# A router that reads the residual itself, and picks its experts with max8 and match-replace, in an encoder layer on one core

## The chip, the cores and the metric

The kernel runs on one core of a Trainium2 chip. The metric is the device time in microseconds (us), the median of a few runs. The engines are TensorE (PE; its weight loads are listed as PEld), VectorE (DVE), ScalarE (ACT), GpSimd (POOL) and SyncE (SP), which here issues all the transfers.

## The reference

One encoder layer over 256 tokens of width 1024: an input projection, a convolution branch and a windowed attention branch, their gated sum, an output projection, and a layer norm; then a mixture of experts and a second layer norm. The change lies at the border between the two halves:

```python
x = layer_norm(DEEPNORM_ALPHA * x + mixed, ln1_g[l], ln1_b[l])
...
g_logits = (t @ w_rg + b_rg).astype(jnp.float32)          # 4 groups
g_prob = jax.nn.softmax(g_logits, axis=-1)
g_idx = jnp.argmax(g_logits, axis=-1)
g_w = jnp.take_along_axis(g_prob, g_idx[:, None], axis=-1)
e_logits = (t @ w_re + b_re).astype(jnp.float32).reshape(-1, N_GROUPS, EXPERTS_PER_GROUP)
e_in = jnp.take_along_axis(e_logits, g_idx[:, None, None], axis=1)[:, 0]
e_prob = jax.nn.softmax(e_in, axis=-1)
top_w, top_i = lax.top_k(e_prob, TOP_K)                   # 2 of the group's 8 experts
top_w = top_w / top_w.sum(-1, keepdims=True)
weight = g_w * top_w
...
for e in range(N_EXPERTS):                                # 32 experts, hidden width 256
    hg, hu = jnp.split(t @ w_gate_up[e], 2, axis=-1)
    out = out + comb[:, e:e + 1] * ((jax.nn.silu(hg) * hu) @ w_down[e])
```

## The kernel before

**Blocks.** The first half is a loop over 72 weight blocks of 128x1024, each loaded by SP into one of four `raw` buffers: 48 of the input projection, 8 each of the attention, convolution and output projections. ScalarE rounds a block to fp32r (`w_hi`, L567), POOL subtracts that from the block (`w_lo`, L502), both in halves of 512 columns into two buffers, and TensorE makes three products for each pair of tiles (hi x hi, hi x lo, lo x hi; L1250 to L1252). VectorE takes finished pairs of blocks out of PSUM. For a convolution pair it multiplies by the gate (L893), adds the attention branch (L897); ScalarE rounds the sum (`a_hi`, L597), in its queue ahead of the split of the next block, and VectorE makes `a_lo` (L899). The eight output blocks (64 to 71) add to four PSUM banks, `out_bank`, into which VectorE has put alpha times the residual (L990). They hold two token tiles t by two column halves c.

**Layer norm and logits.** VectorE takes moments of each bank (L994, L997), ScalarE the root (L675), and the normalised rows z go from the banks to `xt` (L1011 on VectorE, L684 on ScalarE). TensorE turns them (L1412), ScalarE and VectorE copy the result (L679, L1024) and TensorE makes 36 logits a token with router weights scaled by the norm's gain (L1418). Eight products of ones with the shift-scaled weights (L1402) add the shift's part. ScalarE rounds z to `x1_hi` (L693), POOL makes `x1_lo` (L511).

**Routing.** VectorE runs a chain in which each step waits for the one before (`chained`): largest group, the first of equals by a descending key, a mask for other groups, the largest expert by the same five steps (`first_of_largest`), then the second. The sum of the two one-hots (L1070, `onehot_done`) goes to TensorE, which counts for each token how many before it chose each expert, with a strict upper triangle `tri` and a matrix of ones (L1443 to L1447, fp32). From these ranks come each token's place in its expert's list, a 0/1 matrix that gathers the first four experts' tokens (L1079), the weights, the sort of all 512 (token, expert) entries (`compact`), and the start of each expert's list. Then `load_known` releases POOL, which turns z into x1 (L517, L520). `keep_warm` issues products of ones with constants whose results nobody reads.

**Experts.** Sixteen pairs of experts, windows of 64 tokens each: gather (first four experts L1458, the others from the sorted copy), gate-up (L1498), silu (L717), h (L1162), transposes of h (L1522), down (L1533), scatter into `out_bank` (L1548). `build_gather` (L1132, L1137) and `build_scatter` (L1169) on VectorE make 0/1 matrices. SP refills seven homes of gate-up weights and four of down weights as products release them.

## Time and profile before

| What | us |
|---|---|
| Median of 3 runs (lowest, highest) | 487.08 (486.75, 487.19) |
| The profiled execution's own time | 486.77 |
| Its span | 484.6 |
| TensorE busy | 467.1 |
| VectorE busy | 245.6 |
| ScalarE busy | 202.4 |
| POOL busy | 223.2 |
| Last output product ends | 236.25 |
| First gather instruction | 252.53 |
| TensorE's time for a pair of experts, from the chain | 12.94 |

The span runs from the first to the last instruction. In a timeline, a row has the start, the time, the engine, the line, the operation, out<-in, the shapes, the count, and in brackets the idle time before it with what ended it; a matmul's time has its latency in it, so the distance between starts is what one costs. A fp32 product is two instructions. A row of the windows has the stretch, its length, the busy time with count of PE, PEld, DVE, ACT and POOL, then TensorE's granted clock as a share of 2.4 GHz, the DMA engines' busy share and GB/s. Durations of a line are least/median/greatest in ns.

### The profile page before, as it was taken

The numbers are of one execution on the slowest core, as the hardware profiler recorded it, in microseconds if no ns is written. First come the engines' busy times: TensorE is split into PE (matmuls) and PEld (weight loads), VectorE is DVE, ScalarE is ACT, GpSimd is POOL, SyncE is SP. The second block draws the span as 40 slices with busy tenths as digits, with TensorE's granted clock in tenths as the row PEclk, the third lists the DMA queues.
The fourth block names the chain that finished last, engine by engine and source line by source line (L and its number), as shares of the span: only waits on it lengthen the run. The fifth ranks groups of instructions, "written<-read, shape, count | busy, mean of one in ns | idle before, by whom it ended". The sixth has DMA issues, their size and how long they took to land.

```text
span 484.6 us, 7686 instructions
## 1 busy us (share of the span) xinstructions
PE 467.1 (96%) x2816; PEld 329.7 (68%) x2816; DVE 245.6 (51%) x536; ACT 202.4 (42%) x447; POOL 223.2 (46%) x187
## 2 busy tenths in 40 slices
PE   8999999999999999999998999999999999999991
PEld 6999999888999999998884464443334444444431
DVE  2079999759997546560469442222222222222116
ACT  3544455488775687454425241212122222222212
POOL 2898989855866778999235321110001111111002
PEclk9999999999999999999999999999999999999996
DMA  8799989532533354557974999999999999999922
GB/s 291 257 355 378 354 284 360 193 131 88 194 131 121 121 168 156 199 174 277 428 292 164 395 419 381 427 422 421 420 422 421 422 420 422 421 421 421 421 97 88
DMA packets 26370, 145.13 MB, mean 299 GB/s; under 512 B 3040, under 2 KB 3296, under 8 KB 13792
## 3 DMA queue, kind: packets, MB, share of 16 engines
q1 hardware_dynamic: 26336, 144.67, 75.9%
q8 instruction: 23, 0.38, 0.3%
q14 instruction: 11, 0.09, 0.1%
HBM read 143.61 MB, written 1.05 MB: 298 GB/s over the span
## 4 chain that ended last, share of the span: by engine, by line
PE 86%; DVE 6%; ACT 3%; DMA 2%; issue 1%; SPq 1%; POOL 1%; DVEq 0%; ACTq 0%
PE bank L1498 21%; PE bank L1250 13%; PE bank L1252 13%; PE bank L1251 13%; PE bank L1533 12%; PE bank L1548 3%; PE bank L1549 3%; DMA raw<-in_w_in 2%; PE bank L1328 1%; PE bank L1306 1%; PE bank L1522 1%; DVE info L1137 1%; POOL w_lo L502 1%; PE bank L1472 1%; PE bank L1473 1%
## 5 line engine op out<-in xcount | busy, mean ns | idle before, releaser
L502 POOL TENSOR_TENSOR w_lo<-raw,w_hi 128x512 fp32r<-128x512 f32 x140 | 183.1, 1326 | 46.8 <-ACT w_hi L567 43.3
L567 ACT CAST w_hi<-raw 128x512 fp32r<-128x512 f32 x140 | 85.2, 620 | 80.1 <-PE bank L1252 75.6
L1250 PE MATMUL bank<-x_hi,w_hi 128*128 128x256 f32 x400 | 115.4, 289 | 1.3 <-POOL w_lo L502 1.3
L1252 PE MATMUL bank<-x_hi,w_lo 128*128 128x256 f32 x400 | 113.1, 283 | 0.0
L1251 PE MATMUL bank<-x_lo,w_hi 128*128 128x256 f32 x400 | 113.1, 283 | 0.0
L813 DVE SCALAR_TENSOR_TENSOR bank<-slots,par,bank 128x256 f32<-128x256 f32 x232 | 92.3, 481 | 0.2
L528 POOL COPY raw<-gates 128x512 f32 x28 | 19.8, 706 | 153.1 <-PE bank L1498 134.6
L1498 PE MATMUL bank<-slots,raw 128*64 128x512 f32 x320 | 84.5, 592 | 0.0
L1250 PEld LDWEIGHTS bank<-x_hi,w_hi 128*128 128x128 f32 x400 | 76.6, 192 | 2.0 <-issue 1.3
L1251 PEld LDWEIGHTS bank<-x_lo,w_hi 128*128 128x128 f32 x400 | 76.7, 192 | 0.3
L1252 PEld LDWEIGHTS bank<-x_hi,w_lo 128*128 128x128 f32 x400 | 76.7, 192 | 0.0
L1533 PE MATMUL bank<-slots,kT 128*64 128x512 f32 x256 | 58.5, 598 | 0.4 <-ACT kT L723 0.4
L1498 PEld LDWEIGHTS bank<-slots,raw 128*64 128x64 f32 x320 | 27.5, 137 | 44.8 <-issue 44.4
L1162 DVE SCALAR_TENSOR_TENSOR pT<-pT,kT,bank 128x256 f32<-128x256 f32 x16 | 7.7, 481 | 89.6 <-ACT pT L717 89.6
L1176 DVE TENSOR_TENSOR w_lo<-bank,w_hi 128x512 fp32r<-128x512 f32 x32 | 22.1, 691 | 57.2 <-ACT w_hi L730 57.2
L717 ACT ACTIVATE pT<-bank 128x256 f32<-128x256 f32 x16 | 6.1, 384 | 94.2 <-PE bank L1498 94.2
L1533 PEld LDWEIGHTS bank<-slots,kT 128*64 128x64 f32 x256 | 17.2, 136 | 28.3 <-issue 28.1
L730 ACT CAST w_hi<-bank 128x512 fp32r<-128x512 f32 x32 | 18.8, 586 | 36.8 <-PE bank L1533 36.8
L1548 PE MATMUL bank<-w_hi,w_lo 128*128 128x512 f32 x64 | 28.2, 440 | 1.2 <-DVE gates L1183 0.9
L1498 PE MATMUL bank<-spare,raw 128*64 128x512 f32 x64 | 28.1, 592 | 0.0
L1498 PE MATMUL bank<-extra,raw 128*64 128x512 f32 x64 | 28.1, 592 | 0.0
L1498 PE MATMUL bank<-late,raw 128*64 128x512 f32 x64 | 28.1, 592 | 0.0
(213 smaller groups left out, 657.1 us busy)
## 6 DMA issues: line engine op xcount, KB each, us to landing
slots<-in_w_gate_up SPq DMA_DIRECT2D x40, 1024.0 KB, 13.2
slots<-in_w_down SPq DMA_DIRECT2D x32, 1024.0 KB, 13.8
raw<-in_w_in SPq DMA_DIRECT2D x48, 512.0 KB, 4.3
extra<-in_w_gate_up SPq DMA_DIRECT2D x8, 1024.0 KB, 13.2
spare<-in_w_gate_up SPq DMA_DIRECT2D x8, 1024.0 KB, 16.1
late<-in_w_gate_up SPq DMA_DIRECT2D x8, 1024.0 KB, 16.3
raw<-in_w_attn SPq DMA_DIRECT2D x8, 512.0 KB, 3.2
raw<-in_w_conv SPq DMA_DIRECT2D x8, 512.0 KB, 3.3
```

Of the source, the lines that this page charges most:

```text
L502: nc.gpsimd.tensor_tensor(w_lo[:, n % SPLIT, m], raw[:, b % RAW, m], w_hi[:, n % SPLIT, m].bitcast(F32), ALU.subtract).then_inc(w_lo_done, 1)
L528: ins = nc.gpsimd.tensor_copy(xg[u][:, :, j * WIN:(j + 1) * WIN], xgT[:, :, bass.ds(at, WIN)])
L567: nc.scalar.copy(w_hi[:, n % SPLIT, m], raw[:, b % RAW, m]).then_inc(w_hi_done, 1)
L730: nc.scalar.copy(y_hi[:, c * HALF:(c + 1) * HALF], y_bank[c][:]).then_inc(y_hi_done, 1)
L813: ins = nc.vector.scalar_tensor_tensor(dst, h_pad[:, i, tap:tap + SEQ], w, so_far, ALU.mult, ALU.add)
L1176: nc.vector.tensor_tensor(y_lo[:, n], y_bank[c][:], y_hi[:, n].bitcast(F32), ALU.subtract).then_inc(y_lo_done, 1)
L1250: mm(dst, ah, bh, start=first, stop=False, **kw)
L1251: mm(dst, ah, bl, start=False, stop=False, **kw)
L1252: return mm(dst, al, bh, start=False, stop=last, **kw)
L1498: ins = mm(gu_bank[j * WIN:(j + 1) * WIN, :], xg[u][:, k, j * WIN:(j + 1) * WIN], weights(j, k // (KT // 2), k % (KT // 2) == 0)[:, n], st ...
L1533: ins = mm(y_bank[c][j * WIN:(j + 1) * WIN, :], hT[:, k, j * WIN:(j + 1) * WIN], w[:, k, c * HALF:(c + 1) * HALF], start=(k == 0), stop=(k ...
L1548: mm(dst, s, y_hi[:, n], start=False, stop=False, skip_group_check=True)
```

## The change

- The logits are made from the residual sum r itself: the column mean of each scaled router column is taken out of the weights (sums on VectorE, two small products, a subtraction), the shift's part goes into the bias, and VectorE multiplies the logits by each token's inverse deviation. ScalarE copies r from the banks to `xt`; TensorE turns r; ScalarE alone normalises, afterwards. L1402 goes.
- Experts are chosen with one max8 and one match-replace for each token tile. The groups' key is scaled to serve as the mask. Many of the small operands are in PSUM.
- The ranks are products of fp32r operands: two for the ranks of both token tiles, two for the totals.
- The first gather matrix and the first gather go by token tile. The sort moves behind the weights and the first two `build_gather`.
- The constants that this needs (fp32r copies of `tri` and ones, the token numbers in `info`, filling values) are set by VectorE before block 63's pair is taken. Of the warm-up products, 3 at the start stay, 17 become 6.

```diff
-WARM_START, WARM_NORM, WARM_TURN, WARM_ROUTE, WARM_PLACE = 3, 2, 1, 11, 2
+WARM_START, WARM_ROUTE, WARM_PLACE = 3, 5, 1
...
             for t in range(TT):
...
+                for c in range(2):
+                    m = slice(c * HALF, (c + 1) * HALF)
+                    pool.wait_ge(x1_hi_done, 2 * t + c + 1)
+                    nc.gpsimd.tensor_tensor(x1_lo[:, t, m], xt[:, t, m], x1_hi[:, t, m].bitcast(F32),
+                                            ALU.subtract).then_inc(x1_lo_done, 1)
+            pool.wait_ge(x1_lo_done, 2 * TT)
+            pool.wait_ge(gat_built, 2)
             pool.wait_ge(load_known, 1)
...
+            def copy_r(n, t, c):
+                act.wait_ge(out_done, n + 1)
+                nc.scalar.copy(xt[:, t, c * HALF:(c + 1) * HALF], out_bank[2 * t + c][:]).then_inc(r_copied, 1)
+            def copy_rT(n, c):
+                act.wait_ge(r_turned, n + 1)
+                nc.scalar.copy(x1T[:, 4 * c:4 * c + 4, 0:P],
+                               turned_bank[n][:].rearrange("p (a t) -> p a t", a=4)).then_inc(rT_by_act, 1)
+            def normalize_rows(t, c):
+                act.wait_ge(z_shift, t + 1)
+                nc.scalar.activation(xt[:, t, c * HALF:(c + 1) * HALF], out_bank[2 * t + c][:], ACT.Identity,
+                                     scale=mv[:, t, 3:4], bias=mv[:, t, 4:5]).then_inc(z_done, 1)
+            def split_x1(t, c):
+                m = slice(c * HALF, (c + 1) * HALF)
+                nc.scalar.copy(x1_hi[:, t, m], xt[:, t, m]).then_inc(x1_hi_done, 1)
+            nc.scalar.activation(sig[:, 0, 0:1], eps[:, 0:1], ACT.Sqrt)
+            for n, (t, c) in enumerate(((0, 0), (1, 0), (0, 1), (1, 1))):
+                copy_r(n, t, c)
             deviation(0)
...
+            copy_rT(0, 0)
             deviation(1)
...
+            copy_rT(2, 1)
             for t in range(TT):
...
+                if t == 1:
+                    act.wait_ge(r_turned, 2 * TT)
+                for c in range(2):
+                    normalize_rows(t, c)
+                    act.wait_ge(z_done, 2 * t + c + 1)
+                    split_x1(t, c)
             act.wait_ge(exp_in, 1)
+            for t in range(TT):
+                nc.scalar.activation(rt[:, 7, t, :], masked[:, t, 0:EXPERTS], ACT.Exp, bias=rs[:, 2, t:t + 1])
...
+                    chained(nc.vector.tensor_tensor(wr[:], wr[:], per_channel[0], ALU.mult))
+                    for a, w in enumerate((wr[:], bias_wr)):
+                        ins = nc.vector.tensor_reduce(wr_sums[:, a, :], w.rearrange("p k n -> p n k"), X_AXIS, ALU.add)
+                    ins.then_inc(wr_summed, 1)
+                if b == B_CONV - 2:
+                    dve.wait_ge(wr_means_done, 1)
+                    nc.vector.tensor_tensor(wr[:], wr[:], wr_bank[:, 0, :].unsqueeze(1).broadcast_to([P, KT, LOGITS]),
+                                            ALU.subtract)
+                    nc.vector.tensor_tensor(row[:, R_BIAS:R_BIAS + LOGITS], row[:, R_BIAS:R_BIAS + LOGITS],
+                                            wr_bank[:, 1, :], ALU.add).then_inc(wr_ready, 1)
+                if b == B_OUT - 2:
+                    nc.vector.memset(needles, NO_LOGIT)
+                    nc.vector.memset(masked[:, :, EXPERTS:], NO_LOGIT)
+                    for u in range(2):
+                        for n in (0, 5):
+                            nc.vector.tensor_copy(info[u][:, :, n:n + 1], con[:, C_TOKEN:C_TOKEN + TT].unsqueeze(2))
+                    nc.vector.tensor_copy(tri_r, tri)
+                    nc.vector.tensor_copy(ones_r, ones[:]).then_inc(sums_ready, 1)
+                    dve.wait_ge(sums_ready, 1)
                 if b == B_VAR:
...
             for n, (t, c) in enumerate(((0, 0), (1, 0), (0, 1), (1, 1))):
...
+                dve.wait_ge(r_copied, n + 1)
+                moments(t, c, xt[:, t, c * HALF:(c + 1) * HALF])
+            def copy_rT(n, c):
+                dve.wait_ge(r_turned, n + 1)
+                nc.vector.tensor_copy(x1T[:, 4 * c:4 * c + 4, P:2 * P],
+                                      turned_bank[n][:].rearrange("p (a t) -> p a t", a=4)).then_inc(rT_by_dve, 1)
+            copy_rT(1, 0)
             inverse(0)
...
+            shift(0, z_shift)
+            copy_rT(3, 1)
             inverse(1)
...
+            shift(1, z_shift)
             def per_token(col, n):
                 return col.unsqueeze(2).broadcast_to([P, TT, n])
...
             dve.wait_ge(logits_done, 1)
...
+            for t in range(TT):
+                ins = nc.vector.scalar_tensor_tensor(lg[:, t, :], logit_bank[:, t, :], mv[:, t, 3:4],
+                                                     row[:, R_BIAS:R_BIAS + LOGITS], ALU.mult, ALU.add)
+            chained(ins)
             g_log = lg[:, :, 0:GROUPS]
...
             chained(nc.vector.tensor_reduce(rs[:, 0, :], g_log, X_AXIS, ALU.max))
+            for t in range(TT):
+                ins = nc.vector.scalar_tensor_tensor(group_key[:, t, :], g_log[:, t, :], rs[:, 0, t:t + 1], rank4,
+                                                     ALU.is_equal, ALU.mult)
+            chained(ins)
+            chained(nc.vector.tensor_reduce(rs[:, 1, :], group_key, X_AXIS, ALU.max))
+            def grouped(a):
+                return a.rearrange("p (g e) -> p g e", g=GROUPS)
+            for t in range(TT):
+                ins = nc.vector.scalar_tensor_tensor(
+                    grouped(masked[:, t, 0:EXPERTS]), group_key[:, t, :].unsqueeze(2).broadcast_to([P, GROUPS, PER_GROUP]),
+                    rs[:, 1, t:t + 1], grouped(lg[:, t, GROUPS:]), ALU.subtract, ALU.add)
+            chained(ins)
+            for t in range(TT):
+                ins = nc.vector.max(largest[:, t, :], masked[:, t, 0:EXPERTS])
+            chained(ins)
+            chained(nc.vector.tensor_copy(needles[:, :, 0:2], largest[:, :, 0:2]))
+            for t in range(TT):
+                ins = nc.vector.match_replace(marked[:, t, :], needles[:, t, :], masked[:, t, :], NEVER)
+            chained(ins)
+            nc.vector.tensor_scalar(onehot, marked[:, :, 0:EXPERTS], NEVER, None, ALU.is_equal).then_inc(onehot_done, 1)
+            nc.vector.tensor_scalar(rs[:, 2, :], largest[:, :, 0], -1.0, None, ALU.mult)
             nc.vector.tensor_tensor(rg[:, 0, :, :], g_log, per_token(rs[:, 0, :], GROUPS),
...
+            chosen = onehot.bitcast(F32)
+            rank = bank[4][:, 0:TT * EXPERTS].rearrange("p (t n) -> p t n", t=TT)
+            place = rt[:, 0, :, :]
             dve.wait_ge(onehot_done, 1)
             dve.wait_ge(ranks_done, 1)
...
+            chained(nc.vector.scalar_tensor_tensor(first_place, rank[:, :, 0:4], 1.0, chosen[:, :, 0:4], ALU.add, ALU.mult))
+            for t in range(TT):
+                nc.vector.tensor_tensor(
+                    first_places[:, t, :].rearrange("p (j s) -> p j s", j=4),
+                    iota[:, 0:WIN].unsqueeze(1).broadcast_to([P, 4, WIN]),
+                    first_place[:, t, :].unsqueeze(2).broadcast_to([P, 4, WIN]), ALU.is_equal).then_inc(first_built, 1)
+            nc.vector.scalar_tensor_tensor(place, rank, 1.0, chosen, ALU.add, ALU.mult)
+            dve.wait_ge(router_exp, 1)
+            nc.vector.tensor_reduce(rs[:, 6, :], rg[:, 1, :, :], X_AXIS, ALU.add)
+            chained(nc.vector.tensor_tensor(rt[:, 6, :, :], chosen, rt[:, 7, :, :], ALU.mult))
+            chained(nc.vector.tensor_reduce(rs[:, 9, :], rt[:, 6, :, :], X_AXIS, ALU.add))
...
             def build_gather(p, u):
@@ -1199,6 +1217,33 @@
             build_gather(0, 0)
             build_gather(1, 1)
+            dve.wait_ge(ranks_done, 2)
...
+            for t in range(TT):
+                if t == 0:
+                    chained(nc.vector.tensor_reduce(load_f[:], rt[0:1, 9, 0, :], X_AXIS, ALU.max))
+                nc.vector.scalar_tensor_tensor(compact[:, t, :], iota, rs[:, 14, t:t + 1], first_choice[:, t, :],
+                                               ALU.is_equal, ALU.add).then_inc(compact_built, 1)
+            for w in range(WINDOWS + 1):
+                nc.vector.tensor_scalar(starts_f[:, w, :], rt[0:1, 9, 1, :], float(WIN * w), float(ROUTED),
+                                        ALU.add, ALU.min)
+            chained(nc.vector.tensor_copy(load_i[:], load_f[:]))
+            nc.vector.tensor_copy(starts[:], starts_f).then_inc(load_known, 1)
+            dve.wait_ge(load_known, 1)
...
+                if b == B_VAR + 3:
+                    pe.wait_ge(p_copied, HEADS)
+                    pe.wait_ge(wr_summed, 1)
+                    mm(wr_bank[:, 0, :], mean_ones[:], wr_sums[:, 0, :], start=True, stop=True)
+                    mm(wr_bank[:, 1, :], ones[:], wr_sums[:, 1, :], start=True, stop=True).then_inc(wr_means_done, 1)
+            pe.wait_ge(wr_ready, 1)
...
+            def turn_r(n, t, c):
+                pe.wait_ge(r_copied, n + 1)
                 for i in range(4):
...
+                    at = 4 * c + i
+                    ins = nc.tensor.transpose(turned_bank[n][:, i * P:(i + 1) * P], xt[:, t, at * P:(at + 1) * P], ident)
+                ins.then_inc(r_turned, 1)
...
+            turn_r(0, 0, 0)
+            turn_r(1, 1, 0)
+            turn_r(2, 0, 1)
+            pe.wait_ge(rT_by_act, 1)
+            turn_r(3, 1, 1)
             logits(0, 0)
...
+            pe.wait_ge(rT_by_dve, 1)
+            logits(1, 0)
+            pe.wait_ge(rT_by_act, 2)
             logits(0, 1)
...
+            pe.wait_ge(rT_by_dve, 2)
             logits(1, 1).then_inc(logits_done, 1)
             keep_warm(bank[1][:, 0:SEQ], WARM_ROUTE)
...
+            pe.wait_ge(sums_ready, 1)
+            pe.wait_ge(z_done, 2 * TT)
             pe.wait_ge(onehot_done, 1)
...
+            mm(bank[4][:, 0:TT * EXPERTS], tri_r, onehot.rearrange("p t n -> p (t n)"), start=True, stop=False,
+               skip_group_check=True)
+            mm(bank[4][:, EXPERTS:TT * EXPERTS], ones_r, onehot[:, 0, :], start=False, stop=True,
+               skip_group_check=True).then_inc(ranks_done, 1)
+            mm(bank[5][:, 0:EXPERTS], ones_r, onehot[:, 0, :], start=True, stop=False)
+            mm(bank[5][:, 0:EXPERTS], ones_r, onehot[:, 1, :], start=False, stop=True).then_inc(ranks_done, 1)
+            keep_warm(bank[2][:, 0:SEQ], WARM_PLACE, iota[:, 0:SEQ])
...
+                for t in range(TT):
+                    pe.wait_ge(x1_lo_done, 2 * t + 2)
+                    pe.wait_ge(first_built, t + 1)
+                    for k in range(KT):
+                        n = slice(k * P, (k + 1) * P)
+                        dst = first_bank[k // 2][:, (k % 2) * SEQ:(k % 2 + 1) * SEQ]
```

Of long stretches the diff shows the lines that are new or stay; the removed ones stand in the functions above. Not shown either: the places of the new small tensors, the names of semaphores, the last norm, whose moments keep their banks.

## Rows read from the trace of the kernel before

**Rows 1.** The page: the chain that ended last, shares of the span by engine.
```profile
PE 86%; DVE 6%; ACT 3%; DMA 2%; issue 1%; SPq 1%; POOL 1%; DVEq 0%; ACTq 0%
```
**Rows 2.** Windows of the first gather and gate-up; columns as told above.
```profile
252.53:256.53 4.00, 4.00 (x32) 3.87 (x33) 3.52 (x17) 2.77 (x6) 0.00 (x0) 1.00 0.00 0
256.53:263.64 7.11, 7.11 (x34) 2.30 (x33) 6.97 (x22) 2.62 (x5) 3.69 (x2) 1.00 0.32 106
```
**Rows 3.** Timeline of TensorE, 236 to 266 us; columns as told above.
```profile
237.82 1.08 PE L1335 MATMUL bank<-pT,ones 128*128 128x256 f32 x4
238.74 1.04 PE L1412 MATMUL bank<-con,xt 128*128 128x128 f32 x8
...
243.09 1.87 PE L1418 MATMUL bank<-wr,raw 128*128 128x36 f32 x16
244.80 5.00 PE L1335 MATMUL bank<-pT,ones 128*128 128x256 f32 x22
250.02 0.41 PE L1443 MATMUL bank<-rt,con 128*128 128x32 f32 x2 [0.23 <-DVE rt L1070]
...
265.65 0.44 PE L1522 MATMUL bank<-con,pT 128*128 128x128 f32 x2 [1.72 <-DVE pT L1162]
```
**Rows 4.** Timeline of VectorE, routing stretch.
```profile
245.56 0.17 DVE L1039 TENSOR_TENSOR bank<-bank,rs 128x8 f32<-128x8 f32 x1
245.76 0.17 DVE L1040 TENSOR_TENSOR bank<-bank,con 128x8 f32<-128x8 f32 x1
...
246.84 0.22 DVE L1058 TENSOR_REDUCE rs<-rt 128x2 f32<-128x64 f32 x1
247.09 0.22 DVE L1059 TENSOR_TENSOR rt<-rt,rs 128x64 f32<-128x64 f32 x1
...
251.43 0.23 DVE L1077 SCALAR_TENSOR_TENSOR rt<-bank,rt 128x64 f32<-128x64 f32 x1 [1.36 <-PE bank L1447]
```
**Rows 5.** Timeline of ScalarE, routing stretch.
```profile
237.67 0.78 ACT L684 ACTIVATE xt<-bank,mv 128x512 f32<-128x512 f32 x1 [0.79 <-DVE mv L1006]
...
239.37 1.07 ACT L679 COPY raw<-bank 128x512 f32<-128x512 f32 x2 [0.75 <-PE bank L1412]
240.68 0.59 ACT L679 COPY raw<-bank 128x512 f32<-128x512 f32 x1 [0.23 <-PE bank L1412]
...
243.18 1.28 ACT L695 ACT_TABLE_LOAD   x1
```
**Rows 6.** POOL's x1 passes and VectorE beside them; durations of line 511.
```profile
259.95 5.12 POOL L517 TENSOR_TENSOR xt<-xt,gates 128x1024 f32<-128x1024 f32 x2 [12.99 <-DVE starts L1123]
...
260.13 2.40 DVE L1137 CAST info<-weights 128x4 fp32r<-128x4 f32 x2
...
L511 POOL TENSOR_TENSOR x_lo<-xt,x_hi x2: 2348/2352/2357, 242.3 to 244.6; 128x1024 fp32r<-128x1024 f32 x2
```
**Rows 7.** Timelines of VectorE and TensorE around the router scaling and block 55.
```profile
172.23 0.69 DVE L887 TENSOR_TENSOR gates<-bank,gates 128x512 f32<-128x512 f32 x1 [3.12 <-PE bank L1252]
...
187.77 0.39 PE L1250 MATMUL bank<-a_hi,w_hi 128*128 128x256 f32 x1 [0.72 <-POOL w_lo L502]
```
**Rows 8.** Timelines of VectorE and POOL before block 64.
```profile
206.43 1.27 DVE L990 TENSOR_SCALAR bank<-xt 128x512 f32<-128x512 f32 x2
208.67 0.69 DVE L893 TENSOR_TENSOR gates<-bank,gates 128x512 f32<-128x512 f32 x1 [0.97 <-PE bank L1252]
...
212.04 4.06 POOL L502 TENSOR_TENSOR w_lo<-raw,w_hi 128x512 fp32r<-128x512 f32 x3 [0.16 <-ACT w_hi L567]
```
**Rows 9.** Windows: loads in the pair stage, in the gather, at the end.
```profile
300.00:322.00 22.00, 22.00 (x104) 8.76 (x104) 5.69 (x13) 5.05 (x17) 2.26 (x3) 1.00 1.01 422
...
252.00:258.00 6.00, 5.73 (x42) 4.51 (x42) 5.45 (x22) 4.22 (x9) 0.00 (x0) 1.00 0.00 0
...
460.00:464.00 4.00, 4.00 (x22) 1.38 (x20) 0.69 (x1) 0.43 (x1) 0.00 (x0) 1.00 0.81 338
```
**Rows 10.** Window after the last product; timeline of TensorE at the start.
```profile
476.70:484.60 7.90, 0.00 (x0) 0.00 (x0) 5.28 (x11) 1.14 (x3) 2.53 (x2) 0.50 0.36 133
...
4.03 1.87 PE L1347 MATMUL bank<-pT,ones 128*128 128x256 f32 x4
```

229 lines of the change are left out of this document (59 added, 170 removed).

## The prediction

> **What bounds the kernel now.** I first read the page: 86% of the chain that ended last runs on TensorE and 6% on VectorE [rows 1]. Then the windows by stage: TensorE is full in all of them [rows 2], also between 236.25 and 252.53 us. TensorE's timeline shows that this is misleading there: it runs 22 + 4 + 2 + 2 + 4 warm-up instructions (two of the five groups stand in the rows) whose results nobody reads [rows 3]. What really sets that stretch is in VectorE's timeline, which is where its 6% of the chain come from: one small dependent step after another [rows 4]. So TensorE bounds the kernel up to 236.25 (last output product) and again from 252.53 (first gather), and in between lies a serial stretch of 16.28 us. Everything after it hangs on its end: gather 4.00, first gate-up 7.11 [rows 2], then a short wait of 1.72 us before the transposes of h [rows 3], and from there TensorE with next to no idle time. What the change takes out of the 16.28 us therefore comes out of the span, unless another queue is late.
>
> **1. From the last product to the logits.** Before: variance, square root, normalised rows, transposes, logits; VectorE takes the logits at 245.00. After: ScalarE copies the four raw blocks (a PSUM copy is 0.59 us [rows 5]), the fourth from about 236.3 to 236.9. TensorE turns three groups meanwhile (0.44 us each, 1.04 for two with the drain [rows 3]), until 237.6. The fourth needs bank 0 back: moments of the third block (some 0.65 us each in its timeline) end near 236.9, the variance is there at 237.15, ScalarE does the root (0.28) and the copy of the first group (0.59 [rows 5]) until 238.0. Fourth group 238.0 to 238.45. Then the 32 logit instructions, 0.108 us apart (1.87 for sixteen with the drain [rows 3]), 3.45 us, drain 0.2: VectorE starts at 242.1. Gain 2.9. Bounds: if TensorE never waits, 236.25 + 1.75 + 3.45 + 0.2 = 241.65, gain 3.35; if ScalarE's queue is late by one copy and one root, gain 2.0.
>
> **2. The choice.** Before, 245.00 to 250.02: 5.02 us [rows 3, 4]. A dependent step of 8 elements costs 0.20, one of 64 costs 0.26, and a second independent one adds 0.08 to 0.15 [rows 4]. After: logits (a pair) 0.34, group maximum 0.20, key pair 0.28, its maximum 0.20, masked pair 0.33, one-hot 0.25: 1.60 us. Not in this trace: the max8 pair, the copy of two values, the match-replace pair. Lower bound: all three at the price of small steps, 0.28 + 0.20 + 0.28 = 0.76. Upper: ten dependent 64-element steps, 2.5, so that each of the seven instructions stands alone and half of them cost double. I take 1.15 (a reduction of 64 is the nearest row; I count the replace as two instructions each). Together 2.75: onehot at 244.85, gain 2.3 (0.9 to 2.65).
>
> **3. The ranks.** Before, 250.02 to 251.43: ten instructions for five fp32 products, some 0.112 apart [rows 3, 4]. After, VectorE waits for two one-pass products only: 1.41 - 8 x 0.112 = 0.51. Gain 0.9; if each product still were two instructions, 0.7.
>
> **4. First places.** Before, 251.43 to 252.53: 1.10 (all 64 places, then 128x512 in 0.69 us). After: 8 elements 0.22, then 128x256 in 0.40 (L1132 in VectorE's timeline, the same comparison at that size), hand-over 0.08: 0.7. Gain 0.4. The second half is built while TensorE does the first 16 products.
>
> Sum: 2.9 + 2.3 + 0.9 + 0.4 = **6.5 us**; the gather starts near 246.0.
>
> **What could be late next.** ScalarE must normalise and split four halves before TensorE may write the ranks: 4 x (0.78 + 0.6) [rows 5] from 239.05 puts the fourth normal row at 244.0, 0.85 before onehot; its price if slower is one for one. POOL's low parts (a half is 1.16, half of the 2.35 of [rows 6]) end near 245.7, and are needed for the second half of the gather at 248.0. The exponentials (table 1.28, three of 0.2 [rows 5]) end at 246.4; VectorE waits some 0.3 us for them, after the places. ScalarE's first gathered copy comes later (all groups close in the second half, 248.5) but 2 x 0.49 us later is 249.5, before TensorE ends the gather at 250.0. The sort and the token starts, moved behind the weights and the two gather matrices, keep VectorE until about 254.6; h needs it at 265.11 - 6.5 = 258.6. So they are off the path, with 4 us of cover. POOL's four passes over x1, held behind load_known, start near 254.5 instead of 259.95 [rows 6]; the masks they hold up are needed only after the second gate-up.
>
> **5. Work added further up.** The router sums and column means: two reductions of 288 elements after the scaling at 169.1. The nearest rows bound each by 0.22 [rows 4] and 1.43 (L974, 288 elements); VectorE then idles 3.12 us until 172.23 [rows 7]. Hidden; without that cover, up to 2.9. The four small TensorE instructions near 178 (0.45 us) fall ahead of a stall of 0.7 us on TensorE, caused by ScalarE and POOL [rows 7]. Subtracting the means takes under 1 us in VectorE's next idle stretch. Cost 0.
>
> **6. The eight small instructions before block 63.** This is where I expect a loss. Two memsets, four casts of 128x2, and copies of two 128x128 matrices come after VectorE's residual scaling, which ends at 207.70. VectorE next takes a pair of blocks at 208.67, with 0.97 us idle before it [rows 8]. Own time of the eight: 0.75 us. But POOL runs its 1.3 us subtractions back to back. In the gather stretch, two casts of 128x4 took 2.40 us, ending when POOL's 2.56 us pass ended [rows 6], and the next two 2.38; when POOL is idle the pair takes 0.23. So VectorE's copies wait for POOL's running instruction and get a short burst in between. VectorE's lateness goes to the merge at L897, to ScalarE, which holds block 64's split behind a_hi (L597), to POOL's start at 212.04 on block 64, to TensorE at 214.43. POOL's first subtraction there is done 1.08 us before TensorE needs it. With one wait for POOL the merge is 0.3 us later: nothing. With two, 1.9: a stall of 0.9. With three, 2.9: a stall of 1.8; more there cannot be, as POOL has only three subtractions left until ScalarE feeds it. TensorE can't win it back (2.73 us a block against POOL's 2.65). I take two waits, **0.9** (0 to 1.8).
>
> **Rivals.**
> - *As computed*, 481.5, own range 480.4 to 483.0: 0.57.
> - *No stall in part 6*: 487.08 - 6.5 = 480.6. For it: the 0.97 us gap and 1.08 us of slack. Against: the casts. 0.18.
> - *The gain is capped by the expert loads.* The DMA engines are full during the pair stage (share 1.01, and 14.9 us for 6.29 MB at 422 GB/s against 12.94 us of TensorE a pair) [rows 9] (12.94 is how often the chain repeats). If the loads did not move up, only their margin would be won: the last ones land near 463.2, the last down product starts at 469.02; about 5.1 for the gate-up halves ahead of them in the queue, so 482.0. Against: between 252 and 260.2 the DMA engines stand still, and every refill waits for a product that moves up too. 0.05.
> - *VectorE is late for h* because the sort now stands before it: only what exceeds 4 us counts, say 483. 0.03.
> - *TensorE's clock falls for a while.* Of the 34 warm-up instructions 22 are gone, 20 of them between the last product and onehot. The granted clock is 1.00 (2.4 GHz) throughout and 0.50 (1.2 GHz) from 476.7, 4.1 us after the last product [rows 10]; at the half rate an instruction of 256 columns took 0.43 (the start of the run) instead of 0.22 [rows 3, 10]. If it fell at the end of the logits, the ten warm-ups would end at 246.2 instead of 244.1, 1.4 late, and half of the gather would double (+2.0), the whole +4.0. Time 484.9 to 486.9, I take 485.2. The Trainium skill (TensorE: Matmul & The Clock Gate, section "Part 4: PE-mode transpose") says that transposes do not bring the full clock; the trace can't show it, since they have warm-ups among them here. 0.12.
> - *The same, but the clock stays low through the first gate-up*: 1.4 + 4.0 + 7.1 = 12.5 us lost, 6.9 slower net of the gain, 494. It decides from the point where the low clock costs 5.6: the whole gather and over 0.2 us of gate-up. For it: TensorE's gaps of about 0.4, 0.7 and 0.5 us; against: it is never idle for long, and the kernel before kept 1.00 through a gap of 1.72. 0.05.
>
> **Numbers.** The first four cases hold 0.83, between 479.7 (parts 1 and 2 at their best and no stall: 479.8) and 485.2, where the low-clock case begins to weigh; that is the range. Faster by over 0.2%: 0.83 and nine tenths of 0.12: 0.93. Within 0.2%: 0.02. Slower: 0.05.
>
> **What would show it.** First logits instruction on VectorE near 5.8 us after the last product's end (8.75 before); onehot 2.75 after that; places 0.5 after onehot; gather about 9.8 after the last product (16.28 before); the 1.72 us wait before the first transposes of h unchanged; clock row at 1.00 in all of it; a TensorE stall of about 0.9 at block 64, its releaser POOL. The prediction is wrong if that stall exceeds 2 us, if max8 and match-replace together cost over 2.5, or if the clock row falls.

## The result, and the profile after

| What | before | after |
|---|---|---|
| Median, us (lowest to highest, runs) | 487.58 (486.72 to 489.40, 20) | 485.17 (483.43 to 487.13, 20) |
| Ratio, 95% interval | | 0.9947 (0.9937 to 0.9958) |
| Span of the profiled execution | 484.6 | 482.9 |
| Last upstream product over, next instruction starts | 236.09 | 239.83 |
| First logits instruction on VectorE | 245.00 | 246.01 |
| First rank product | 250.02 | 249.48 |
| First gather instruction | 252.53 | 250.85 |

The change makes the kernel faster by 0.53% (0.42 to 0.63), 2.6 us, of the 5.6 forecast (2.6 goes by the ratio; the two medians lie 2.4 apart). The forecast time of 481.5 is 3.7 below the median; 0.5 of that comes from before's own median, which was 487.08 in the three runs of the forecast and is 487.58 in twenty. The stretch behind the last upstream product did shrink, from 16.44 to 11.02 us between the starts of its first instruction and of the gather, but it begins 3.74 us later. (The prediction counts from 236.25, where the chain has the end of the product; below it is always the start of the next instruction, 236.09.)

**The routing stretch.** The page's chain by engine now has half the share of VectorE that it had [rows 1]:
```profile
PE 90%; DVE 3%; ACT 3%; DMA 1%; issue 1%; POOL 1%; DVEq 0%; SPq 0%; ACTq 0%
```
TensorE's timeline after the last product, to be laid beside [rows 3]:
```profile
239.83 1.47 PE L1455 MATMUL bank<-con,xt 128*128 128x128 f32 x12
241.75 0.66 PE L1455 MATMUL bank<-con,xt 128*128 128x128 f32 x4 [0.45 <-ACT raw L703]
242.25 3.66 PE L1461 MATMUL bank<-wr,raw 128*128 128x36 f32 x32
245.74 4.09 PE L1380 MATMUL bank<-pT,ones 128*128 128x256 f32 x10
249.48 0.38 PE L1481 MATMUL bank<-onehot,sums 128*128 128x64 f32 x1
```
Three groups of raw transposes, a wait of 0.45 for bank 0, the fourth group, 32 logits instructions: 6.18 us to VectorE's first step, where it was 8.91. Then ten warm-up instructions take 4.09 us; at the full clock ten take 2.40 (in before_few_warm's profile). They are the first sign of something that the forecast's sum puts at zero.

VectorE's timeline of the choice and the hand-over to the ranks, against [rows 4]:
```profile
246.01 0.43 DVE L1089 SCALAR_TENSOR_TENSOR bank<-bank,mv,row 128x36 f32<-128x36 f32 x2 [2.53 <-PE bank L1461]
246.47 0.17 DVE L1093 TENSOR_REDUCE rs<-bank 128x2 f32<-128x8 f32 x1
...
247.70 0.29 DVE L1109 MAX8 bank<-rt 128x8 f32<-128x32 f32 x2
248.03 0.16 DVE L1111 COPY rt<-bank 128x4 f32<-128x4 f32 x1
248.22 0.09 DVE L1113 MATCH_VALUE_LOAD bank<-rt 128x8 f32 x1
248.30 0.19 DVE L1113 MATCH_REPLACE8 bank<-rt 128x40 f32<-128x40 f32 x1
...
248.70 0.23 DVE L1115 TENSOR_SCALAR onehot<-bank 128x64 fp32r<-128x64 f32 x1
...
250.07 0.17 DVE L1125 SCALAR_TENSOR_TENSOR bank<-bank,onehot 128x8 f32<-128x8 f32 x1 [1.01 <-PE bank L1483]
```
The new instructions are cheap: both maxima, the copy and both replacements run from 247.70 to 248.70. One-hot is done at 248.93, 2.92 after the first step; with the hand-over TensorE could have started at 3.05 (the kernel late_consts_warm_logits, where it waits for one-hot, shows that). It starts at 249.48 since the warm-ups ahead of the rank products in its queue are still running.

The windows of the routing, the gather and the first gate-up [rows 2]:
```profile
239.83:250.85 11.02, 10.43 (x66) 9.05 (x64) 7.03 (x32) 9.42 (x18) 5.06 (x4) 0.85 1.01 424
250.85:254.85 4.00, 4.00 (x34) 3.87 (x34) 3.62 (x21) 1.34 (x3) 0.00 (x0) 1.00 0.85 352
254.85:262.00 7.15, 7.15 (x35) 2.34 (x34) 3.68 (x16) 3.89 (x8) 3.06 (x2) 1.00 0.35 113
```
Gather and gate-up cost what they did, 4.00 and 7.15 us. The mean clock of the first stretch is 0.85; a finer window shows where it goes:
```profile
244.00:246.00 2.00, 2.00 (x19) 2.00 (x19) 0.00 (x0) 1.97 (x4) 1.83 (x2) 0.96 1.00 422
246.00:249.50 3.50, 3.50 (x11) 2.76 (x10) 2.77 (x18) 3.41 (x6) 3.23 (x3) 0.54 1.01 414
```
From 245.84 on TensorE is granted 1.2 GHz, half, for 3.41 us: the choice's warm-ups and nothing else. In before's profiled execution it had 2.4 GHz up to its last product.

**Where the 3.74 us come from.** Part of it was there from the beginning. Groups of TensorE in the first 25 us, of after, and of the same kernel in another profiled execution (after_again):
```profile
L1317 PE MATMUL bank<-gates,raw 128*128 128x256 f32 x32 | 9.0, 450 | 0.7 <-DMA raw<-in_w_in 0.7
```
```profile
L1317 PE MATMUL bank<-gates,raw 128*128 128x256 f32 x32 | 7.2, 382 | 0.8 <-DMA raw<-in_w_in 0.8
```
The same 32 instructions take 1.8 us more in one execution of one and the same kernel. At block 55 after is 1.41 us behind before (189.18 against 187.77, [rows 7]), after_again 0.23: that is the start, and no part of the change. The rest, 3.74 - 1.41 = 2.33 us, arises at block 64. VectorE's and POOL's timelines of after, which answer to [rows 8] (w_lo x3 are the three subtractions on block 64):
```profile
207.85 1.27 DVE L1047 TENSOR_SCALAR bank<-xt 128x512 f32<-128x512 f32 x2
209.09 1.27 DVE L1028 CAST info<-con 128x2 fp32r<-128x2 f32 x1
209.12 0.07 DVE L1024 MEMSET rt<- 128x16 f32 x1
209.13 0.07 DVE L1025 MEMSET rt<- 128x16 f32 x1
210.28 1.42 DVE L1028 CAST info<-con 128x2 fp32r<-128x2 f32 x3
211.61 1.33 DVE L1029 CAST sums<-con 128x128 fp32r<-128x128 f32 x1
212.86 0.21 DVE L1030 CAST sums<-ones 128x128 fp32r<-128x128 f32 x1
213.11 0.69 DVE L930 TENSOR_TENSOR gates<-bank,gates 128x512 f32<-128x512 f32 x1
```
```profile
215.83 4.68 POOL L517 TENSOR_TENSOR w_lo<-raw,w_hi 128x512 fp32r<-128x512 f32 x3 [2.98 <-ACT w_hi L585]
```
And TensorE's first product of block 64, in before and in after:
```profile
214.23 0.40 PE L1250 MATMUL bank<-w_hi,a_hi 128*128 128x512 f32 x1
```
```profile
217.25 0.47 PE L1295 MATMUL bank<-w_hi,a_hi 128*128 128x512 f32 x1 [1.45 <-POOL w_lo L517]
```
Six casts and copies that together are worth some 0.6 us fill 4.0 us: three of them end a POOL subtraction later than they could. The two memsets between them take 0.07 each. The Trainium skill (SBUF — State Buffer, section "Who interferes with whom") has copies and casts in a two-port mode waiting while GpSimd holds the ports that they share, and an instruction outside these modes with at most one input from SBUF, as a memset is, not waiting; the rows agree with both halves. VectorE takes the pair of blocks at 213.11; less the 1.41 of the start that is 3.0 later than the 208.67 of before. POOL's three subtractions on block 64 start 2.4 later by the same count and take 4.68 instead of 4.06 us.

### The profile page after: what moved, and what is told of

Same layout as the page of the kernel before. It is cut to its first block, busy times and chain, and to the rows that moved or that the text cites. A ratio compares the mean times of both kernels' runs of the same rounds, so it can differ in the third digit from the quotient of the medians.

```text
span 482.9 us, 7627 instructions
## 1 busy us (share of the span) xinstructions
PE 464.1 (96%) x2776; PEld 326.1 (68%) x2776; DVE 242.2 (50%) x538; ACT 207.2 (43%) x457; POOL 222.9 (46%) x189
## 4 chain that ended last, share of the span: by engine, by line
PE 90%; DVE 3%; ACT 3%; DMA 1%; issue 1%; POOL 1%; DVEq 0%; SPq 0%; ACTq 0%
PE bank L1539 23%; PE bank L1295 13%; PE bank L1297 12%; PE bank L1296 12%; PE bank L1574 12%; PE bank L1589 4%; PE bank L1590 3%; PE bank L1317 2%; PE bank L1373 1%; PE bank L1351 1%; DMA raw<-in_w_in 1%; PE bank L1563 1%; DVE stat L1051 1%; POOL w_lo L517 1%; PE bank L1380 1%
```

## The experiments

All of them were run with five rounds beside the kernel before. "Last product" is where the instruction after the last upstream product starts, less the lag at block 55 against before (187.77), so that the start of the execution is out of it: before has 236.09, after 238.42, a stall of 2.33.

**1. late_consts.** The change, with the eight instructions moved behind VectorE's work on the last block.
```diff
-                if b == B_OUT - 2:
-                    nc.vector.memset(needles, NO_LOGIT)
...
-                    nc.vector.tensor_copy(ones_r, ones[:]).then_inc(sums_ready, 1)
-                    dve.wait_ge(sums_ready, 1)
+            dve.wait_ge(w_lo_done, 2 * splits_before(N_BLOCKS))
+            nc.vector.memset(needles, NO_LOGIT)
...
+            nc.vector.tensor_copy(ones_r, ones[:]).then_inc(sums_ready, 1)
+            dve.wait_ge(sums_ready, 1)
```

> The changed kernel, but VectorE's eight small instructions (two memsets, four casts, two 128x128 copies) no longer stand before block 63's pair; they run after the block loop, once POOL has made its last low part, and nothing else differs. Theory (VectorE's casts wait for POOL's running subtraction, three in a row, and ScalarE holds block 64's split behind the merge): TensorE's two stalls at blocks 64 and 65 (1.4 and 1.1 us) go, the output product ends some 2.3 us earlier counted from the first split block, and the ratio to the kernel before goes from 0.9947 to about 0.990. Rival (the stall has another cause, such as the w_out loads or the router means further up): the stalls stay and so does the ratio, 0.9947.

483.04 us, ratio 0.9914 (0.9889 to 0.9939). Its last product is at 236.21 - 0.16 = 236.05: the stall is gone to the last tenth. (The second stall of 1.1 us that the expectation puts at block 65 is the one that ends at 121.0; it is in before as well, at 119.60.) VectorE's timeline at the new place, where POOL has no subtraction left:
```profile
233.49 0.15 DVE L1044 CAST info<-con 128x2 fp32r<-128x2 f32 x1
233.50 0.07 DVE L1041 MEMSET rt<- 128x16 f32 x1
233.54 0.30 DVE L1044 CAST info<-con 128x2 fp32r<-128x2 f32 x3
233.75 0.22 DVE L1045 CAST sums<-con 128x128 fp32r<-128x128 f32 x1
```
The same instructions take what their size costs. The median is 2.1 below that of after, by the ratios it is 1.6, and their intervals just overlap (0.9939 and 0.9937); the row of the last product is the surer sign. The clock is no better here, as two windows show:
```profile
240.90:247.60 6.70, 6.70 (x24) 5.86 (x23) 2.77 (x18) 5.32 (x10) 4.67 (x4) 0.50 1.01 416
247.70:251.00 3.30, 3.16 (x25) 2.79 (x24) 2.63 (x13) 0.00 (x0) 0.00 (x0) 1.00 0.98 407
```
Here the clock is at half for the second half of the logits and all of the choice. The 32 logits instructions took 4.81 us, against 3.66 at the full clock in after.

**2. before_with_consts.** The kernel before with nothing but the eight instructions, in the change's place.
```diff
...
+                if b == B_OUT - 2:
+                    nc.vector.memset(spare_rt[:, 0:16], 0.0)
+                    nc.vector.memset(spare_rt[:, 16:32], 0.0)
+                    for u in range(2):
+                        for n in (0, 5):
+                            nc.vector.tensor_copy(info[u][:, :, n:n + 1], con[:, C_TOKEN:C_TOKEN + TT].unsqueeze(2))
+                    nc.vector.tensor_copy(sums_sb[:, 0, :], tri)
+                    nc.vector.tensor_copy(sums_sb[:, 1, :], ones[:]).then_inc(sums_ready, 1)
+                    dve.wait_ge(sums_ready, 1)
```

> The kernel before with only those eight instructions added before block 63's pair (their results are not used). Theory: they alone cost 2.3 us, ratio 1.0047, with VectorE's casts lasting to the ends of POOL's subtractions and TensorE stalled at block 64. Rival (they only hurt together with the rest of the change): ratio 1.000.

490.70 us, ratio 1.0057 (1.0036 to 1.0078), 2.8 us slower. Last product 238.75 - 0.34 = 238.41: a stall of 2.32, with nothing else of the change there. So the stall belongs to these eight instructions alone, and nothing behind it wins it back: the interval of the time is 1.8 to 3.8 us. The profiled execution also has 3.41 us at half the clock from 269.13 on, behind the wait of 1.72 us ahead of the transposes of h, which before's own profile has not.

**3. four_casts_early.** The change with only the four casts in that place; memsets and the two 128x128 copies stand late as in experiment 1.

> The changed kernel with only the four casts of the information rows left ahead of block 63; the three memsets-and-copies of the 128x128 constants stand behind the block loop. Theory A (each cast or copy on VectorE that falls between POOL's pieces waits for one of them, and the run of POOL pieces is what is late for TensorE): two POOL waits instead of three, the last upstream product ends 0.7 to 1.2 us later than without any of them (the changed kernel: 2.3), ratio to the kernel before 0.991 to 0.993. Theory B (any instruction in that place costs the whole stall, because VectorE then comes behind the next POOL piece): stall 2.3 as in the changed kernel, ratio 0.995. Theory C (the copies are what costs, since they read and write more): stall 0 to 0.4, ratio 0.990.

483.87 us, ratio 0.9923 (0.9900 to 0.9946). VectorE's timeline:
```profile
206.46 1.27 DVE L1042 TENSOR_SCALAR bank<-xt 128x512 f32<-128x512 f32 x2
207.65 2.60 DVE L1026 CAST info<-con 128x2 fp32r<-128x2 f32 x4
210.16 0.68 DVE L930 TENSOR_TENSOR gates<-bank,gates 128x512 f32<-128x512 f32 x1
```
and TensorE's:
```profile
214.77 0.47 PE L1297 MATMUL bank<-w_hi,a_hi 128*128 128x512 f32 x1 [0.36 <-POOL w_lo L517]
```
Two waits, and a last product at 237.20 - 0.02 = 237.18: a stall of 1.09. No wait gives 0, two give 1.1, three 2.3 (one alone was not run). The number of waits decides (A); not the place alone (B), and not the copies alone (C).

**4. after_again.** The changed kernel once more, on the same chip as 3, 7 and 8.

> The changed kernel itself, unchanged, on the same chip as the others. Ratio to the kernel before 0.993 to 0.996; TensorE waits for POOL's w_lo pieces 3.0 to 3.5 us in the block loop; whether the clock is full early in the span or some 4 us later should move its span by about 1.4 us; if the late start belongs to the change, it will be late here too, and if it is chance, it can be at 5 to 6 us.

484.31 us, ratio 0.9933 (0.9910 to 0.9956), consistent with the first comparison. Last product 238.70 - 0.23 = 238.47: stall 2.38. Its start was the early one, its clock fell too, for 3.41 us from 245.05. So the late start differs between executions of one kernel, and the other two losses came in both profiles.

**5. before_few_warm.** The kernel before with the change's numbers of warm-up products.
```diff
-WARM_START, WARM_NORM, WARM_TURN, WARM_ROUTE, WARM_PLACE = 3, 2, 1, 11, 2
+WARM_START, WARM_NORM, WARM_TURN, WARM_ROUTE, WARM_PLACE = 3, 0, 0, 5, 1
```

> The kernel before with the changed kernel's number of warm-up products and nothing else: none around the norm and the transposes, five after the logits, one after the ranks. Clock theory (with few products among transposes and narrow logits the granted clock falls near the end of the logits): the clock row shows under 1.00 between 240 and 252 us, warm-ups of 0.43 us an instruction, and where the fall reaches the gather some us are lost; ratio 1.000 to 1.008. Removing 10 of them from the way before the logits saves up to 0.9 us by itself, ratio 0.998, if the clock stays. Rival (the fall in the changed kernel comes from its order of work, not from the number of warm-ups): clock 1.00 throughout.

489.14 us, ratio 1.0031 (1.0015 to 1.0048). Windows of its choice and gather:
```profile
248.00:252.00 4.00, 1.82 (x12) 1.41 (x12) 2.40 (x11) 0.20 (x1) 0.00 (x0) 1.00 0.72 297
252.00:255.40 3.40, 3.35 (x16) 3.39 (x17) 2.95 (x15) 1.02 (x2) 0.00 (x0) 0.50 0.01 2
255.40:258.00 2.60, 2.60 (x21) 2.18 (x22) 2.53 (x9) 2.28 (x5) 0.00 (x0) 1.00 0.00 0
```
TensorE stood idle for 2.97 us before the ranks, and the clock falls in the gather: 16 instructions in 3.4 us where the next 2.6 us have 21. Fewer warm-ups do cost the clock, in the old kernel as well: six of the twelve runs have a mean clock of 0.982 to 0.986, where the lowest of the 18 runs of before beside them is 0.989. The time is 1.5 us longer (0.7 to 2.3).

**6. late_consts_warm_logits.** Experiment 1 with three single warm-up products: one in the 0.45 us wait ahead of the fourth transposes, two among the logits.
```diff
             turn_r(2, 0, 1)
+            keep_warm(bank[7][:, SEQ:2 * SEQ], 1)
             pe.wait_ge(rT_by_act, 1)
...
             logits(1, 0)
+            keep_warm(bank[1][:, 0:SEQ], 1)
             pe.wait_ge(rT_by_act, 2)
             logits(0, 1)
+            keep_warm(bank[1][:, 0:SEQ], 1)
             pe.wait_ge(rT_by_dve, 2)
```

> The kernel of late_consts with three warm-up products more: one in TensorE's 0.45 us gap before the fourth group of transposes, two among the logits. They lengthen the way to the logits by 0.9 us. Clock theory: if three are enough, the clock row stays at 1.00, the ten warm-up instructions after the logits take 2.2 instead of 4.1 us, TensorE is ready before onehot, and the loss of 0.9 is partly given back (0.5): ratio 0.4 us above late_consts, with less spread between runs. Rival (the clock has nothing to do with it or three are too few): the clock falls all the same and the ratio is 0.9 us, 0.002, above late_consts.

483.13 us, ratio 0.9900 (0.9882 to 0.9919), and the narrowest spread so far: 482.90 to 483.50 in five runs, against 482.58 to 485.53 in experiment 1. Its windows:
```profile
236.20:248.00 11.80, 10.72 (x75) 9.26 (x74) 7.47 (x35) 9.42 (x18) 5.09 (x4) 1.00 1.01 421
262.00:266.00 4.00, 4.00 (x12) 1.39 (x10) 4.00 (x5) 0.87 (x3) 3.50 (x3) 0.57 1.02 426
```
Full through the routing, and low for 3.41 us after the next wait, the 1.77 us ahead of the first transposes of h.

**7. late_consts_route3.** Experiment 1 with 3 instead of 5 warm-up products in the choice (6 instructions instead of 10).

> late_consts with 3 warm-up products in place of 10 between the logits and the choice's result. Theory A (the ten products at the low clock run past the choice and hold the ranks up by about half a us, and the clock is bought back by nothing they do): the rank products start when onehot is there, 0.3 to 0.6 us sooner, ratio 0.989 to 0.991. Theory B (those products keep the clock up for the gather): TensorE is idle some 1.5 us there, the low stretch comes in the gather or the transposes of h, the time is the same as late_consts or up to 1.5 us longer, ratio 0.991 to 0.995.

485.03 us, ratio 0.9932 (0.9908 to 0.9955): worse than experiment 1 by 2.0 us in the medians and by 0.9 in the ratios, whose intervals overlap. Seven of its eight runs have a mean clock of 0.983 to 0.985; experiment 1 has 0.984 to 0.991. Windows:
```profile
243.00:253.00 10.00, 9.55 (x37) 8.29 (x37) 6.78 (x39) 4.84 (x9) 4.16 (x4) 0.50 0.96 396
253.00:256.00 3.00, 3.00 (x22) 2.32 (x23) 2.82 (x10) 2.21 (x5) 0.00 (x0) 1.00 0.02 8
```
The ranks did start sooner, 3.05 us after VectorE's first step instead of 3.75. But the low stretch is now 10.24 us long and takes most of the gather with it. Theory A, that those products do nothing but stand in the ranks' way, does not hold. (The 10 in this expectation and in the first one of experiment 8 counts instructions, which are 5 products; the 3 and the 7 beside it count products.)

**8. late_consts_filled**, and once more on another chip as **late_consts_filled_again**. Experiment 6 with 7 products in the choice and three in the wait ahead of the transposes of h.
```diff
-WARM_START, WARM_ROUTE, WARM_PLACE = 3, 5, 1
+WARM_START, WARM_ROUTE, WARM_PLACE = 3, 7, 1
...
             slot_info(0, 0)
+            keep_warm(bank[2][:, 0:SEQ], 3, iota[:, 0:SEQ])
             for p in range(PAIRS):
```

> late_consts_warm_logits with 7 warm-up products in place of 10 in the choice and 3 more in the 1.8 us in which TensorE waits ahead of the transposes of h. Theory A (the low stretch at 262 us comes from the idle time just before it): no stretch at 0.5 until the end, the transposes of h and the first gate-up products take 1 to 1.7 us less, span 480.0 to 480.6, ratio 0.987 to 0.989. Theory B (the low stretch is not tied to that gap): there is one at another place, and the ratio stays at 0.990 as in late_consts_warm_logits.

> late_consts_filled once more, on the chip of the two kernels beside it. Ratio 0.987 to 0.990; the runs in two groups about 1.4 us apart if the clock at the start decides, the lower one at 481.8, the larger.

481.90 us, 0.9889 (0.9866 to 0.9913), and 481.64 us, 0.9888 (0.9868 to 0.9907). Both profiles have no stretch at half the clock before the last product. The window that was at 0.57:
```profile
262.00:266.00 4.00, 4.00 (x20) 1.55 (x18) 4.00 (x5) 1.46 (x4) 3.59 (x3) 1.00 1.04 432
```
20 instructions in the same 4 us instead of 12. The low stretch came from the wait just before it, and the runs agree: 481.4 to 482.0 in eight of twelve, the other four 482.8 to 483.1, as the two starts would have it.

**9. before_gap_filled.** The kernel before with those three products ahead of the transposes of h.

> The kernel before with one addition: 3 warm-up products in the 1.7 us in which TensorE waits ahead of the first transposes of h. Theory A (the runs of the kernel before near 488.2 to 488.8 us are those in which the clock falls at that wait, those near 486.9 the ones in which it does not): nearly all runs at 486.6 to 487.1, ratio 0.997 to 0.998. Theory B (the upper group comes from the start of the kernel, where the clock becomes full some 4 us later in some executions, at a price of 1.4 to 1.6 us): both groups stay, ratio 0.999 to 1.001.

487.05 us, ratio 0.9988 (0.9976 to 1.0001). The runs lie in two groups as those of the kernel before do: 486.6 to 487.5 (9 runs) and 488.1 to 488.5 (3), against 486.5 to 487.0 (6) and 488.1 to 488.9 (11). Fewer in the upper group, but the group is not gone, so the late start (B) is one cause of it. This profile is such a case: the first 32 products took 8.9 us, there was no low stretch after them, and the last product was at 237.46.

Theory A is not out altogether. Of the 59 runs of the kernel before that were taken beside these experiments 18 have a mean clock of 0.989 or less, and all 18 lie above 488.4; of the 12 filled runs none is under 0.992. A mean of 0.989 is, as an estimate, 10.7 us at half the clock, and the end of the kernel has 4.8 to 8.1 us of it in the fourteen profiles, so these runs had another low stretch somewhere. Where, they do not show; before_with_consts had its own right behind this wait. So the upper group is made of late starts and, probably, of falls. What the fill is worth is not settled.

**10. after_filled.** The changed kernel, its eight instructions where the change has them, with all the fills of experiment 8.

> The changed kernel, its eight small instructions where the change puts them, with only the warm-up products of late_consts_filled (7 in the choice, three single ones ahead of and among the logits, 3 ahead of the transposes of h). Theory A (stall and clock are two separate losses that add): the last upstream product ends 2.3 to 2.6 us later than in late_consts_filled and nothing else differs; ratio 0.993 to 0.9945, no stretch at 0.5 between the start and the last product. Theory B (the clock is low because TensorE stood still at block 64 before it, so that without the stall there is no clock loss): a stretch at 0.5 shows up again here near 245 us in spite of the fills, ratio 0.995 to 0.996.

484.88 us, ratio 0.9945 (0.9925 to 0.9964). Last product 238.45 - 0.08 = 238.37, a stall of 2.28, and 3.2 us above late_consts_filled_again on the same chip. The clock is full in the profile in spite of the stall, and the mean clock is 0.993 to 0.995 in all six runs, so the stall alone does not bring it down (against B). Yet the kernel gains nothing measurable over the plain change. TensorE's timeline shows the price of the fills:
```profile
240.87 1.87 PE L1461 MATMUL bank<-wr,raw 128*128 128x36 f32 x16
242.57 0.68 PE L1380 MATMUL bank<-pT,ones 128*128 128x256 f32 x2
243.09 0.98 PE L1461 MATMUL bank<-wr,raw 128*128 128x36 f32 x8
243.90 0.68 PE L1380 MATMUL bank<-pT,ones 128*128 128x256 f32 x2
```
TensorE is busy among the logits, so each product put there takes 0.43 to 0.5 us of its time: 7.05 us from the last product to VectorE's first step instead of 6.18. That is 0.87 us, about what the clock is worth.

**11. late_consts_two_fills_less.** Experiment 8 without those two.

> late_consts_filled without the two warm-up products among the logits (the one in TensorE's wait ahead of the fourth transposes, the 7 in the choice and the 3 ahead of the transposes of h stay). Theory A (each of the two takes TensorE's time, 0.43 us, and the clock does not need them): logits on VectorE 6.2 us after the last upstream product's end instead of 7.05, clock at 1.00 until the last product, ratio 0.987. Theory B (they are what keeps the clock full in the logits and the choice): a stretch at 0.5 shows up between 240 and 250 us in the profile or the runs spread by over 2 us, ratio 0.989 to 0.991.

480.96 us, ratio 0.9873 (0.9840 to 0.9905), the lowest median of all. Five of the six runs lie at 480.75 to 482.15, one at 485.23. The profiled one is the 482.15, and has both sides in it:
```profile
237.50:239.50 2.00, 1.98 (x17) 1.58 (x16) 1.91 (x7) 1.86 (x4) 0.00 (x0) 1.00 1.02 426
239.50:241.67 2.17, 2.17 (x22) 2.17 (x21) 0.21 (x1) 2.11 (x5) 1.27 (x1) 1.00 1.01 423
241.67:245.08 3.41, 3.41 (x12) 2.87 (x12) 2.27 (x15) 3.33 (x5) 3.28 (x3) 0.50 1.01 416
```
In this execution the clock fell in the logits, although the wait ahead of the fourth transposes was filled and TensorE's rows have no wait between 206 us and the fall; the mean clock of the four runs at 480.75 to 481.00 is 0.993 to 0.994, that of this one 0.990, that of the 485.23 0.988. So those products are worth the clock in some executions (B) and cost up to 0.9 us (A): 480.9 when it goes well, against 481.6 to 481.9 in experiment 8. Which is better over many runs six can't say.

## Why the prediction was wrong

The direction was right; the size was forecast at 5.6 us and measured at 2.6. Two of the three signs of being wrong that it named came: a stall over 2 us and a fall of the clock; the third, a slow max8 and match-replace, did not. The steps, in the prediction's order (clock apart):

| Step | forecast | measured |
|---|---|---|
| 1. last product to logits | +2.9 | +2.73 (8.91 to 6.18) |
| 2. the choice | +2.3 | +1.97 (5.02 to 3.05) |
| 3. the ranks | +0.9 | +0.82 (1.41 to 0.59) |
| 4. first places | +0.4 | +0.32 (1.10 to 0.78) |
| 5. router means further up | 0 | 0: lag 1.40 at 121.0, 1.41 at 189.18 |
| 6. eight instructions at block 63 | -0.9 | -2.33 |
| clock | 0 | -0.4 in the profile; about -1.1 in the medians |

**Step 6 failed.** Its mechanism held: casts wait for POOL's running instruction, the wait moves to the merge, to ScalarE's split, to POOL's start on block 64 and to TensorE. "I take two waits, 0.9 (0 to 1.8)" went wrong twice. The count was three (two did give 1.09), and 1.8 was said to be the most there can be. With three, POOL starts 2.4 us late and the first product of block 64 starts 1.61 late (217.25 less 1.41, against 214.23). So POOL's lateness was absorbed by 0.8 and not by 1.08: before's first subtraction took 1.55 and ended at 213.59, only 0.64 ahead of that product. The other 0.72 is what the bound left out. It comes within block 64, at whose end the lag is 2.33: POOL's three subtractions take 4.68 instead of 4.06 us, and TensorE, which used to have one in hand, follows each as it comes. The first took 1.27, the next two some 1.75 each (1.30 and 1.29 before), and VectorE's own late work on the same block, at 216.59 and 218.39, lies beside these two; that this is why they are slower is read from the rows, no run sets it apart. A chain that has used up its slack pays for every later lateness as well. VectorE's rows of after show the six going in pairs, with one wait for each pair. Three was therefore to be had from [rows 6], where each pair of casts had waited once.

**The clock.** The rival "TensorE's clock falls for a while" named 485.2 and the median is 485.17, but this agreement is an accident: nearly half of the shortfall is step 6 and a fifth is steps 1 to 4. The sum itself had put the clock at 0. What came true is the event. It fell in the choice, not for the whole gather, and cost 0.4 us there (ranks at 249.48 instead of 249.06). In the medians it costs more, since executions differ: the plain change has mean clocks of 0.983 to 0.992 and a spread of 3.7 us. The rest of the sum says 5.6 - 2.6 = 3.0 short, less 0.7 in steps 1 to 4, less 1.4 in step 6: 0.9. A second way: experiment 11's median plus the stall, 480.96 + 2.33 = 483.3, is the change at the full clock (its fastest run is 483.43), so 1.9 us lie between that and its median; before has 0.7 between its lower group, 486.9, and its median. That leaves 1.2. The two agree on about 1 us, not better. The warm-up count the change gives up is the likely reason: experiments 5, 6, 7 and 8 move the low stretch about, or away, by warm-up products alone, and all twelve runs of experiment 8 have a mean clock of 0.992 or more. It is not the whole of it, since before_with_consts with all its warm-ups and experiment 11 with its wait filled had a fall too. One reading made the clock look steadier than it is: the prediction puts the fall at the end 4.1 us after the last product, but products of the scatter run until 475.22, 1.5 us before it.

**Steps 1 to 4** were each somewhat too high: 5.84 us measured, 6.5 forecast. In step 2 the unknown instructions were right (1.00 us against 1.15 taken); the small known steps were too cheap, 1.69 us up to the first maximum where 1.35 had been counted, since a pair cost 0.35 to 0.43 and not 0.28 to 0.34. Step 5 and the rivals of the late sort, the expert loads and a slower routing table did not happen: the wait ahead of h is 1.77 (was 1.72).

As a check of the whole: without the stall and with the clock full, experiment 11 has 480.9 in four runs and the lower group of before 486.9, 6.0 us apart. That agrees with the 5.84 of steps 1 to 4, though experiment 11 has a few warm-ups more than the change; the stall takes 2.3 of it and the clock about 1.

## What to carry to other kernels

Small setup copies are not small where they stand beside a busy POOL: count one POOL instruction for each pair of them, then follow the lateness through every queue, and when the slack is gone add the later pieces too; put them where POOL is idle, which was worth 2.3 us here for no other edit. When a serial stretch is shortened, its dummy work on TensorE has to be laid out anew: in its waits it is free (one product in 0.45 us, three in 1.8 us), among real work it costs its own time. A kernel whose runs lie in groups should be compared group by group, or the 1.4 us of the start are taken for the edit's.

## What the runs showed of the hardware

- The clock fell to 1.2 GHz in the middle of TensorE's work: at 245.84 in after, when TensorE had run transposes and products of 36 columns for 6 us with one wait of 0.45 us among them. The stretches at 0.50 ahead of the last product were 3.41 us long in seven profiles, once 6.83 and once 10.24. They came after short waits (0.45), after long ones (1.77, 2.97), and in late_consts_two_fills_less after none. The wait of 1.72 ahead of the transposes of h had one behind it in before_with_consts and none in before's own profile. So a wait was neither needed for a fall nor enough for one.
- In the first 10 us of the span the granted clock is recorded as 1.00 while instructions of 256 columns go at half the rate; the full rate came near 5.7 us in some executions and near 10.3 us in others. Windows of after and of after_again over the same stretch:
```profile
5.70:10.30 4.60, 3.90 (x10) 2.95 (x10) 2.45 (x2) 1.76 (x2) 0.00 (x0) 1.00 1.02 385
```
```profile
5.70:10.30 4.60, 3.77 (x17) 3.15 (x17) 2.41 (x2) 1.89 (x2) 0.00 (x0) 1.00 1.02 388
```
  10 instructions against 17, under the same 1.00 in the clock column: there the count tells the rate and the column does not. It moved block 55 by 1.4 to 1.7 us, and three of the fourteen profiles have it (after, late_consts_route3, before_gap_filled). What decides it was not tried.
- VectorE's max8 on 128x32 took 0.15 us, loading eight values to match 0.09 and the replacement over 128x40 0.19: each no more than about one dependent small step of [rows 4].
